# A Hymba and PEER decoder layer on one core: 59 instead of 56 ready-made u tiles

## What is computed

```
h    = rms(x, attn_norm_g);  proj = h @ w_in            # 2048 x 6144: q, k, v, B, C, xc
x    = x + concat(diff_attention(q, k, v), short_conv(B, C, xc)) @ w_out
h2   = rms(x, ffn_norm_g);   q = h2 @ w_q               # 8 heads, two halves of 128
s1, i1, s2, i2 = top 16 of q0 @ subkeys0, q1 @ subkeys1 # 128 keys each
top, experts   = top 16 of the 256 sums s1 + s2;  gates = softmax(top)
act  = gelu(sum_d u[experts, d] * h2[d]) * gates        # u, v: 16384 x 2048
x    = x + sum_k act[k] * v[experts[k]]
```

## Time and profile before

| | |
|---|---|
| three runs | 2951.82, 2954.48 (median), 2954.94 us |
| profiled execution | 2953.46 us, of it the span of the profile 2951.7 |
| busy, share of the span | TensorE 98%, VectorE 80%, GpSimd 52%, ScalarE 36% |
| granted TensorE clock, mean | 0.998 |
| ready-made tiles loaded in the sweep | 56, ordinary ones 72 |
| a store of a turned quarter (256 KB), issue to landing | 7.0 us, median |
| a load of near rows, of far rows (1 MB) | 8.1 and 9.2 us |
| DMA share at 760 to 765, 765 to 770, 775 to 780 us | 0.95, 0.80, 0.05 |

### The profile page before, as it was taken

How to read it: one execution, slowest core, us unless ns; L and a number is a source line. 1 busy time by engine, 2 the same in 40 slices (tenths; PEclk the granted TensorE clock), 3 DMA queues, 4 the chain that set the end, 5 groups by cost and what they waited for, 6 DMA issues and landing times.

```text
span 2951.7 us, 40402 instructions
## 1 busy us (share of the span) xinstructions
PE 2885.2 (98%) x14993; PEld 2566.0 (87%) x14993; DVE 2356.0 (80%) x3050; ACT 1054.8 (36%) x1375; POOL 1540.0 (52%) x906
## 2 busy tenths in 40 slices
PE   7999999999999999999999999999999999999998
PEld 6888777788899999999999999999997777777776
DVE  6455677755678888988888898899777999898998
ACT  4122343341333333434333343334233333333332
POOL 1000232300006766665756666577867878877852
PEclk9999999999999999999999999999999999999999
DMA  8998777779758998999999899999999999999998
GB/s 302 328 353 276 252 240 247 227 295 316 242 177 310 347 334 302 341 322 336 316 319 333 304 336 323 337 336 365 333 352 401 413 416 412 417 418 418 419 417 357
DMA packets 324223, 980.65 MB, mean 332 GB/s; under 512 B 62756, under 2 KB 179504, under 8 KB 240752
## 3 DMA queue, kind: packets, MB, share of 16 engines
q1 hardware_dynamic: 179488, 508.60, 46.4%
q0 software_dynamic: 107008, 439.75, 41.4%
q10 hardware_dynamic: 37584, 30.43, 3.2%
HBM read 866.33 MB, written 112.33 MB: 332 GB/s over the span
## 4 chain that ended last, share of the span: by engine, by line
PE 68%; DVE 13%; DMA 10%; issue 5%; ACT 2%; POOL 1%; ACTq 0%; DVEq 0%; SPq 0%; POOLq 0%
PE ps L1863 21%; PE ps L1865 21%; PE ps L1864 21%; DMA v_two<-in_peer_v 9%; PE ps L2104 3%; DVE x_rows L1713 2%; DVE v_lo L1762 2%; ACT v_hi L1216 2%; DVE u_row L1704 1%; DVE x_one L1811 1%; DVE uT_lo L1672 1%; DMA v_ring<-in_peer_v,experts 1%; DVE uT_lo L1677 1%; PE ps L1946 1%; PE ps L1962 1%
## 5 line engine op out<-in xcount | busy, mean ns | idle before, releaser
L1863 PE MATMUL ps<-hT_hi,uT_hi 128*128 128x384 f32 x2048 | 698.5, 341 | 5.1 <-DVE uT_lo L1672 2.3
L1865 PE MATMUL ps<-h2T_lo,uT_hi 128*128 128x384 f32 x2048 | 686.1, 335 | 0.0
L1864 PE MATMUL ps<-hT_hi,uT_lo 128*128 128x384 f32 x2048 | 684.9, 334 | 0.0
L852 POOL DMA_INDIRECT gate_grid<-gates,grid_cells x256 | 533.7, 2085 | 105.8 <-issue 78.6
L1863 PE MATMUL ps<-v_hi,a_hi 128*128 128x512 f32 x1024 | 403.5, 394 | 34.9 <-DVE v_lo L1762 34.2
L1216 ACT ACTIVATE v_hi<-v_two 128x2048 fp32r<-128x2048 f32 x126 | 241.4, 1919 | 445.9 <-PE ps L1865 306.1
L1864 PE MATMUL ps<-v_hi,a_lo 128*128 128x512 f32 x1024 | 400.5, 391 | 0.0
L1865 PE MATMUL ps<-v_lo,a_hi 128*128 128x512 f32 x1024 | 400.3, 391 | 0.0
L1863 PEld LDWEIGHTS ps<-hT_hi,uT_hi 128*128 128x128 f32 x2048 | 384.8, 188 | 13.5 <-DVE uT_lo L1677 6.6
L1864 PEld LDWEIGHTS ps<-hT_hi,uT_lo 128*128 128x128 f32 x2048 | 385.0, 188 | 1.9
L1865 PEld LDWEIGHTS ps<-h2T_lo,uT_hi 128*128 128x128 f32 x2048 | 384.4, 188 | 0.0
(11 more groups left out here) (209 smaller groups left out, 4975.8 us busy)
## 6 DMA issues: line engine op xcount, KB each, us to landing
v_two<-in_peer_v SPq DMA_DIRECT2D x63, 2048.0 KB, 11.8
u_tile<-in_peer_u SPq DMA_DIRECT2D x72, 1024.0 KB
u_tile<-uT_all SPq DMA_DIRECT2D x56, 1024.0 KB
near_rows<-in_peer_u SPq DMA_DIRECT2D x40, 1024.0 KB, 8.1
uT_all<-near_turned SPq DMA_DIRECT2D x100, 256.0 KB, 7.0
w_raw<-in_w_in SPq DMA_DIRECT2D x24, 1024.0 KB, 9.2
wc_raw<-in_w_in SPq DMA_DIRECT2D x48, 512.0 KB, 6.6
far_rows<-in_peer_u SPq DMA_DIRECT2D x16, 1024.0 KB, 9.2
```

The costliest lines, as they stand in the source:

```text
L852: pool.indirect_dma_start(out=gate_grid, out_offset=bass.IndirectOffsetOnAxis(ap=grid_cells[:, d, col:col + 1], axis=0), in_=gates[:, 2 + ...
L1863: mm(out, a_hi, b_hi, start=first, stop=False)
L1864: mm(out, a_lo, b_hi, start=False, stop=False)
L1865: return mm(out, a_hi, b_lo, start=False, stop=last)
```

## The change

Three more tiles are prepared. One is a far tile in the projections' last chunk: SyncE loads its rows where it stopped before, VectorE turns it between the splits of quarter 2 and the near tile, and SyncE stores it behind the first two `wc_raw` loads. Two are in the output projection's last chunk: a near tile, and one more far tile behind the split of quarter 3. There VectorE now turns near, then far, ahead of the split of quarter 3, and again far behind it. The transfer `w_peer_first` moves in SyncE's queue to between the last two far tiles. In the sweep tiles 113, 115 and 117 are now loaded ready-made.

```
--- before.py
+++ after.py
@@ -75,9 +75,9 @@
 NEAR_HEADS = NEAR_QKV + 2
 KEPT_BY_POOL = 1 + 2 * (HEADS - 1)
 NEAR_OUT = NEAR_HEADS + KEPT_BY_POOL
-NEAR_TURNED = NEAR_OUT + 1 + 3 * (OUT_CHUNKS - 2)
-FAR_QKV = 2 * (QKV_CHUNKS - 1)
-FAR_TURNED = FAR_QKV + 2 * (OUT_CHUNKS - 1)
+NEAR_TURNED = NEAR_OUT + 2 + 3 * (OUT_CHUNKS - 2)
+FAR_QKV = 2 * (QKV_CHUNKS - 1) + 1
+FAR_TURNED = FAR_QKV + 2 * (OUT_CHUNKS - 1) + 1
 TURNED = NEAR_TURNED + FAR_TURNED
 ZERO_DMAS = 2 * HEADS
 EPS = 1e-6
@@ -537,7 +537,7 @@
                     chunk(c)
                 c = QKV_CHUNKS - 1
                 load_wi(c, 0)
-                keep_turned(FAR, 2 * c - 1, last=True)
+                keep_turned(FAR, 2 * c - 1)
                 load_wi(c, 1)
                 keep_turned(NEAR, 3 * c)
 
@@ -573,8 +573,12 @@
                 load_wo(c, 0)
                 keep_turned(FAR, far(c - 1))
                 load_wo(c, 1)
-                keep_turned(NEAR, near(c - 1), last=True)
-                keep_turned(FAR, far(c) - 1, last=True)
+                keep_turned(NEAR, near(c - 1))
+                keep_turned(NEAR, near(c) - 2, last=True)
+                keep_turned(FAR, far(c) - 1)
+                sp.wait_ge(w_ready, 4 * (QKV_CHUNKS + OUT_CHUNKS) - 1)
+                sp.dma_start(w_peer_first[:, :, :], w_q_v[:, :, 0:HALF]).then_inc(wq_in[0], 16)
+                keep_turned(FAR, far(c), last=True)
 
             for t in range(TB):
                 sp.dma_start(x_rows[:, t, :], x_v[t]).then_inc(x_in[t], 16)
@@ -596,6 +600,7 @@
             sp.wait_ge(h_ready, TB)
             conv_piece(0, 0)
             conv_piece(0, 1)
+            keep_turned(FAR, FAR_QKV - 1, last=True)
             for n in range(2):
                 keep_turned(NEAR, NEAR_QKV + n)
             with sp.Fori(0, CT - 1) as j:
@@ -631,8 +636,6 @@
             load_mix(MIX_ORDER[2])
             load_mix(MIX_ORDER[3])
             load_out_weights()
-            sp.wait_ge(w_ready, 4 * (QKV_CHUNKS + OUT_CHUNKS) - 1)
-            sp.dma_start(w_peer_first[:, :, :], w_q_v[:, :, 0:HALF]).then_inc(wq_in[0], 16)
             for t in range(TB):
                 sp.wait_ge(out_done[t], OUT_CHUNKS)
             sp.dma_start(w_peer0[:, :, :], w_q_v[:, :, HALF:2 * HALF]).then_inc(wq_in[1], 16)
@@ -1375,6 +1378,7 @@
             with dve.Fori(1, chunks - 1) as c:
                 qkv_chunk(c)
             split_wi(chunks - 1, 2)
+            turn_rows(FAR, FAR_QKV - 1, "qkv")
             turn_rows(NEAR, NEAR_QKV, "qkv")
             split_wi(chunks - 1, 3)
             turn_rows(NEAR, NEAR_QKV + 1, "qkv")
@@ -1550,8 +1554,10 @@
                 turn_rows(NEAR, 3 * c + (NEAR_OUT - 1), "out")
                 rest_of_chunk(c)
             split_wo(chunks - 1, 2)
+            turn_rows(NEAR, NEAR_TURNED - 1, "out")
+            turn_rows(FAR, FAR_TURNED - 2, "out")
+            split_wo(chunks - 1, 3)
             turn_rows(FAR, FAR_TURNED - 1, "out")
-            split_wo(chunks - 1, 3)
 
             def split_wq(h, c, first=0, end=4, early=False):
                 if first == 0:
```

## The result

The changed kernel takes 2976.84 us (median of 4 runs, 2973.74 to 2979.49), the kernel before 2954.64 (4 runs, 2951.82 to 2954.94). The ratio is 1.0077, with a 95% interval of 1.0064 to 1.0089: 22 us slower. The prediction was slower too, but by 6.4 us only, and 2976.84 lies outside its range of 2953.5 to 2967.

The account below looks back on a forecast made before the run. The prediction took TensorE, busy 2885.2 of 2951.7 us, to bound the kernel. Sweep -4.3, projections 0 and output projection's end +10.7 summed to +6.4 us, so 2961 us, with a range of 2953.5 to 2967.

Parts of the forecast that it names:

- GpSimd's lag: Last head of the sweep: GpSimd doesn't follow the shorter intervals, late gathers cost +1.0 us, bounds 0 and 5.3.
- Part 2, cost 0: Projections' last chunk: the added far tile costs 0, or 3 us without cover.
- 4 us of cover remain: Projections' last chunk: ScalarE's split moves to 272, VectorE takes it up only at 278.73.
- Part 1, gain: Sweep: three ready-made tiles shrink six intervals from 10.10 to 9.22 us, 5.3 us off TensorE's path.
- Rival 2: Last head: GpSimd's 10.09 us a tile swallow nearly all of the 5.3 us gain, 2964.7 us; chance 0.14.
- Part 3, the tail: End of the output projection: two more tiles delay w_peer_first and the first query, +9.0 + 1.7 = +10.7 us.
- the clock's 1.7 us: End of the output projection: TensorE stands 4.8 us, its clock falls, +1.7 us on the path, bounds 0 and 4.
- the signs named: w_peer_first issued near 777, near tile at 767 to 770, first query at 808 to 811, six intervals of 9.2 us.
- The sign of being wrong: First query by 804, or sweep's tile 127 ending less than 2 us earlier against the sweep's start than before.

Follow-up runs that it names:

- e1: Kernel before plus only the far tile in the projections' last chunk (57 ready-made): 2959.20 us.
- e9: As e1, but the far tile's four stores carry a sixteenth of its columns and the sweep doesn't use the tile: 2955.03 us.
- e11: As e9, with the load of the far tile's rows also cut to a sixteenth: 2952.93 us.
- e4: Kernel before, nothing more prepared, but tiles 113, 115 and 117 loaded as ready-made from the stored rows of 107, 109 and 111: 2956.59 us.
- e2: Kernel before plus only the output projection's two tiles (58 ready-made): 2964.09 us.
- e5: As e4, with GpSimd's scatters in the last head spread over 13 tiles instead of 11: 2960.78 us.
- e6: Changed kernel plus 36 matmuls, result unused, in TensorE's wait at the end of the output projection: 2977.81 us.

## Why the prediction was wrong

The sign and the term of the tail were right. Two terms that I held small were not, the far tile of the projections (0 for +6.3 us) and GpSimd's lag (+1.0 for +7.3), and 5.3 us of the profiled execution lie in the dense stage, which the sum did not have.

- **Part 2, cost 0: failed, +6.3 us.** The step that failed is "4 us of cover remain". I followed one wait, ScalarE's for the far stores, and that one came as expected (273.32 for 272). I didn't follow what else is in the DMA queues with the far tile's load and stores, or behind them in SyncE's queue: the first near tile began 2.3 us later, the near stores went out from 270.60, not 267.75, and into full queues, the second near tile began 4.3 us later, and the next `wc_raw` pieces behind it. That TensorE has no idle time in this window was true; the wait came some 25 us later, and ended at 304.22. The 278.73 that I took for a fixed point was itself the end of such a chain: the earlier trace rows show 4.62 us of waiting for near stores ahead of the near tile before it. e1 shows the cost alone, e9 and e11 that it is the bytes.
- **Part 1, gain: right in kind.** Expected -5.3, measured -4.4 in the changed kernel, -4.1 in e4, -2.4 for two tiles and -1.4 for one. The missing part lies in the interval of tile 115 (9.75 to 10.09 us, not 9.22) and in that of tile 112, the head's first (9.64).
- **Part 1, GpSimd's lag: failed, +7.3 instead of +1.0.** I took its 10.09 us for five issues at full speed that simply don't follow. But this number belongs to a pattern that repeats with TensorE's 10.10: in the kernel before the same issues lie over VectorE's dot and addition in each of seven cycles (from 2076.97), and the five add up to 8.6 us. Once GpSimd is late, others do, they add up to 8.4 to 11.1, and the cycle becomes 11.2 us on average (nine cycles from 2094.37 to 2195.10): the lag doesn't stay as it is, it grows by 1 us a tile. With two ready tiles the cycle stays at 10.0 to 10.1 us (e2), with three it doesn't. Rival 2 had the mechanism and the wrong price, since I bounded it by the gain (5.3); it gave back more than was won. The bound was the error: a late engine can cost more than its lag. That the number of issues sets the pace is shown by e5; that their meeting VectorE's instructions makes them long is read from the rows.
- **Part 3, the tail: right, +11.9 for +10.7, but in part by luck: two errors in it offset each other.** The near tile came 15.4 us after the one before (expected 16.0). From there to `w_peer_first` it was 10.6 us, not 8.4 (3.91 us for four far stores, where 2.8 were taken), so that the transfer went out 1.6 us later than expected. Landing and the two splits took 1.1 us more. That makes 2.7 us too little in the queue's part. Against that the clock's 1.7 us fell away: TensorE stood even longer than expected (7.96 us, not 4.8) and the clock fell to 0.61, but on work that waits anyway (e6). What the Trainium skill states ("TensorE: Matmul & The Clock Gate", section "What's actually happening") agrees with the fall, only its price here is nothing; and the second idle time, 1.82 us ahead of the first query, brought no fall (1.00 from 816 to 824 us).
- **The dense stage, +5.3 us, was not in the sum.** In the profiled executions it lasts 751.5 us before and 756.9 after, but 751.5 in e6, whose sweep and dense stage have the changed kernel's code, and 750.9 to 755.4 in the others. The changed kernel's four spans go from 2971.9 to 2977.7, and the profiled one is the longest. I take this part for spread between executions, of which the medians (22.2 us, not 26.0) leave out a good part; that is not shown, and what makes the stage differ wasn't tried.
- **Of the signs named,** `w_peer_first`, the near tile and the first query came as described, but 6.3 us later, which is part 2's error, and four of the six short intervals are 9.2 us long. The sign of being wrong, that tile 127 ends less than 2 us earlier against the sweep's start, came true: it ends 2.4 us later.

## What to carry to other kernels

An idle stretch of the DMA queues may be someone's slack: before 1 or 2 MB are put there, follow each transfer that is issued behind them to its first reader, and that reader's next one, not only the wait that the edit itself adds. An engine that fills its cycle with no wait is no clock that keeps its rate: if its instructions get longer when they meet another engine's, being late by one tile can cost more than the lag. Look for durations that repeat exactly from tile to tile as a sign of a locked pattern, and try how many short tiles it bears.

## What was not expected of the hardware

- The issue of one gather on GpSimd lasts 0.93 to 1.01 us alone and up to 3.13 where it meets a dot or an addition of VectorE; with it the five issues of a tile take between 8.4 and 11.1 us.
- One megabyte more of stores and one of loads, among transfers that share the queues at 300 to 400 GB/s, cost 7.7 us in one place, and 0.6 us were left when both were a sixteenth as large.
- TensorE at a granted clock of 0.61 for 10 us cost nothing where VectorE set the pace, and 4.60 us of wait with a clock of 0.50 and 0.68 behind it were on the path in another.
